# Feed-forward matmuls of a two-block Conformer kernel: one stationary operand for 512 moving columns, gate and up spread over four PSUM banks

## The reference, cut to what matters

```python
def swiglu(h, wg, wu, wd):
    return (jax.nn.silu(h @ wg) * (h @ wu)) @ wd

# first block:    x = x + first_mixer(rms_norm(x)); h = rms_norm(x, norm2_g)
#                 x = x + swiglu(h, w_gate, w_up, w_down)                  first feed-forward
# second block, each of two layers l:
#   x = x + 0.5 * rmsnorm(swiglu(rmsnorm(x, g[0]), ...), g[1])             second, fourth
#   x = x + rmsnorm(mixer(rmsnorm(x, g[2])), g[3])                         even mixer, odd mixer
#   x = x + 0.5 * rmsnorm(swiglu(rmsnorm(x, g[4]), ...), g[5])             third, fifth
```

## Time and profile before

| | before |
|---|---|
| median of 3 runs | 1394.74 us (1394.70 to 1394.78) |
| the profiled execution, its own time | 1394.34 us |
| its span, first to last instruction | 1392.5 us |
| TensorE matmuls | 1361.8 us busy, 98% of the span, 9546 of them |
| VectorE | 774.1 us, 56% |
| ScalarE | 630.3 us, 45% |
| mean granted TensorE clock | 0.992 |
| the 16 DMA engines | 169 GB/s on average |

### The profile page before, as it was taken

The page is one execution under the profiler, slowest core; times in us unless marked ns, Lnnn a source line. Parts: engine busy times, 40 slices in busy tenths (PEclk is TensorE's granted clock), DMA queues, the critical chain, the costliest instruction groups (busy, mean ns, idle before and its releaser), DMA issues.

```text
span 1392.5 us, 22880 instructions
## 1 busy us (share of the span) xinstructions
PE 1361.8 (98%) x9546; PEld 1260.9 (91%) x9546; DVE 774.1 (56%) x906; ACT 630.3 (45%) x811; POOL 86.3 (6%) x117
## 2 busy tenths in 40 slices
PE   8989999999999999999899999999999999999998
PEld 7977999999999999897799999999999998899997
DVE  6976654445644447666754444654445534654443
ACT  6654444443444334545554443454434654543331
POOL 3540000000000000000000000000002120000000
PEclk9999999999999999999999999999999999999999
DMA  8423565554655544224565555555555743465530
GB/s 266 152 91 132 188 211 181 181 182 166 212 182 185 188 145 152 92 86 134 195 221 182 181 183 179 189 204 181 185 192 170 228 119 98 166 234 190 181 121 31
DMA packets 174219, 235.17 MB, mean 169 GB/s; under 512 B 5359, under 2 KB 154111, under 8 KB 174144
## 3 DMA queue, kind: packets, MB, share of 16 engines
q1 hardware_dynamic: 170368, 223.52, 47.6%
q0 software_dynamic: 3184, 9.37, 2.2%
q10 hardware_dynamic: 592, 1.19, 0.2%
HBM read 233.03 MB, written 1.05 MB: 168 GB/s over the span
## 4 chain that ended last, share of the span: by engine, by line
PE 87%; DVE 7%; issue 2%; ACT 2%; POOL 1%; DMA 0%; DVEq 0%; POOLq 0%; ACTq 0%
PE psum L983 27%; PE psum L984 26%; PE psum L985 26%; DVE w_lo L1519 2%; PE psum L1162 1%; PE psum L1154 1%; PE psum L1153 1%; PE psum L1064 1%; DVE psum L1742 1%; ACT ws L438 1%; POOL st L857 1%; PE psum L1170 1%; PE psum L1172 1%; PE psum L1171 1%; DVE ws L1576 1%
## 5 line engine op out<-in xcount | busy, mean ns | idle before, releaser
L1519 DVE TENSOR_TENSOR w_lo<-raw,w_hi 128x2048 fp32r<-128x2048 f32 (+1 forms) x212 | 476.5, 2285 | 73.4 <-ACT w_hi L419 73.4
L983 PE MATMUL psum<-t_hi,w_hi 128*128 128x256 f32 x1472 | 419.1, 285 | 1.6 <-DVE t_lo L1586 1.6
L984 PE MATMUL psum<-t_lo,w_hi 128*128 128x256 f32 x1472 | 417.6, 284 | 0.0
L985 PE MATMUL psum<-t_hi,w_lo 128*128 128x256 f32 x1472 | 417.5, 284 | 0.0
L419 ACT ACTIVATE w_hi<-raw 128x2048 fp32r<-128x2048 f32 (+1 forms) x212 | 396.8, 1900 | 26.9 <-PE psum L985 19.7
L983 PEld LDWEIGHTS psum<-t_hi,w_hi 128*128 128x128 f32 x1472 | 283.6, 193 | 3.6 <-DVE t_lo L1586 1.9
L984 PEld LDWEIGHTS psum<-t_lo,w_hi 128*128 128x128 f32 x1472 | 283.6, 193 | 1.4
L985 PEld LDWEIGHTS psum<-t_hi,w_lo 128*128 128x128 f32 x1472 | 283.5, 193 | 0.0
L983 PE MATMUL psum<-w_hi,t_hi 128*128 128x256 f32 (+2 forms) x912 | 269.6, 296 | 5.3 <-DVE t_lo L1586 3.0
L985 PE MATMUL psum<-w_hi,t_lo 128*128 128x256 f32 (+2 forms) x912 | 265.4, 291 | 0.0
L984 PE MATMUL psum<-w_lo,t_hi 128*128 128x256 f32 (+2 forms) x912 | 265.3, 291 | 0.0
(11 more groups left out here) (166 smaller groups left out, 934.9 us busy)
## 6 DMA issues: line engine op xcount, KB each, us to landing
raw<-in_ffn_wg SPq DMA_DIRECT2D x44, 1024.0 KB, 5.2
raw<-in_ffn_wu SPq DMA_DIRECT2D x44, 1024.0 KB, 6.3
raw<-in_ffn_wd SPq DMA_DIRECT2D x44, 1024.0 KB, 6.5
raw<-in_even_w_in SPq DMA_DIRECT2D x13, 1024.0 KB, 5.2
raw<-in_odd_w_in SPq DMA_DIRECT2D x12, 1024.0 KB, 5.7
raw<-in_w_gate SPq DMA_DIRECT2D x11, 1024.0 KB, 5.2
raw<-in_w_up SPq DMA_DIRECT2D x11, 1024.0 KB, 6.3
raw<-in_w_down SPq DMA_DIRECT2D x11, 1024.0 KB, 6.7
```

The costliest lines, as they stand in the source:

```text
L983: nc.tensor.matmul(o, lh, rh, start=start, stop=False)
L984: nc.tensor.matmul(o, lh, rl, start=False, stop=False)
L985: return nc.tensor.matmul(o, ll, rh, start=False, stop=stop)
L1519: nc.vector.tensor_tensor(w_lo[:, n % SLOTS, 0:w], raw[:, n % RAWS, 0:w], w_hi[:, n % SLOTS, 0:w].bitcast(F32), ALU.subtract).then_inc(lo_ ...
```

## The change

In the chunks 2 to 9 the two matmuls that share the stationary `w_hi` become one whose moving operand is `t_hi` and `t_lo` side by side (they now lie in one tile, `t_both`): 256 + 256 columns into one whole bank. The third (`w_lo` by `t_hi`) adds to the bank's first half. So each 128-channel block has a bank of its own with two halves that still have to be added: gate takes banks 4 and 5, up takes 6 and 7, for every chunk. ACT copies the second halves to SBUF, DVE adds the first halves; silu and product then read SBUF. TensorE waits for the sum of gate (up) of chunk c-1 before it writes gate (up) of chunk c. The three splits of a chunk now stand between these steps in ACT's and DVE's programs and no longer ahead of them. In chunks 0, 1 and 10 gate and up of a chunk become one moving operand of 512 columns, for one token tile, into one bank; `turn_x` stands in the middle of the second pair.

```diff
-        t_hi = sb("t_hi", [P, KT, S], F32R)
-        t_lo = sb("t_lo", [P, KT, S], F32R)
+        t_both = sb("t_both", [P, 2, KT, S], F32R)
+        t_hi, t_lo = t_both[:, 0, :, :], t_both[:, 1, :, :]
...
+        WIDE = CHUNKS - 3
...
+            def halves_of(b):
+                v = psum[:, b:b + 2, :]
+                return v[:, :, 0:S], v[:, :, S:2 * S]
```

ScalarE's part of a chunk, and the end of its program:

```diff
+                def chunk(c, turn=0):
+                    s, k = n0 + 3 * c - 1, WIDE * ph["f"] + c - 1
                     act.wait_ge(unit_used, s + 1 + turn * SLOTS)
-                    nc.scalar.activation(f_s[:, c % 2, :], bank[4 + 2 * (c % 2)][:, :], ACT.Silu).then_inc(silu_done, 1)
-                    act.wait_ge(prod_done, 1 + PARTS * ph["f"] + c + 1 + turn * 2)
+                    nc.scalar.activation(f_b[:, 0, :, :], halves_of(4)[1], ACT.Copy).then_inc(gate_part, 1)
+                    split_hi(s + 3, turn=turn)
+                    act.wait_ge(gate_sum, k + turn * 2)
+                    nc.scalar.activation(f_s[:, c % 2, :], f_s[:, c % 2, :], ACT.Silu).then_inc(silu_done, 1)
+                    split_hi(s + 4, turn=turn)
+                    act.wait_ge(unit_used, s + 2 + turn * SLOTS)
+                    nc.scalar.activation(f_b[:, 1, :, :], halves_of(6)[1], ACT.Copy).then_inc(up_part, 1)
+                    split_hi(s + 5, turn=turn)
+                    act.wait_ge(prod_done, 1 + c0 + c + 1 + turn * 2)
                     nc.scalar.activation(f_hi[:, c % 2, :], f_p[:, c % 2, :], ACT.Copy).then_inc(prodhi_done, 1)
...
-                split_to(n0 + 29)
-                chunk(n0 + 3 * (CHUNKS - 3) - 1, CHUNKS - 3)
-                split_to(n0 + 3 * (CHUNKS - 2) + 5)
-                chunk(n0 + 3 * (CHUNKS - 2) - 1, CHUNKS - 2)
+                chunk(CHUNKS - 3)
+                chunk(CHUNKS - 2)
+                cur[0] = n0 + 3 * CHUNKS - 1
                 split_to(n0 + 3 * CHUNKS + 2)
                 last_silu(0)
```

TensorE:

```diff
+            def by_channels_wide(n, b, turn=0):
+                pe.wait_ge(lo_done, n + 1 + turn * SLOTS)
+                wh, wl = w_cols(n)
+                for c in range(2):
+                    o = bank[b + c]
+                    for k in range(KT):
+                        cs = slice(c * P, (c + 1) * P)
+                        if k < KT - 1:
+                            nc.tensor.matmul(o[:, :], wh[:, k, cs], t_both[:, :, k, :], start=k == 0, stop=False)
+                        nc.tensor.matmul(o[:, 0:S], wl[:, k, cs], t_hi[:, k, :], start=False, stop=False)
+                    mm = nc.tensor.matmul(o[:, :], wh[:, KT - 1, cs], t_both[:, :, KT - 1, :], start=False, stop=True)
+                mm.then_inc(unit_used, 1)
...
+            def by_tokens_pair(n, b, t, between=None):
+                pe.wait_ge(lo_done, n + 2)
+                ts = slice(t * P, (t + 1) * P)
+                for k in range(KT):
+                    tile_ready(t, k)
+                    if between and k == KT // 2:
+                        between()
+                    mm = three(bank[b][:, :], t_hi[:, k, ts], t_lo[:, k, ts], pair_cols(w_hi, n, k), pair_cols(w_lo, n, k),
+                               k == 0, k == KT - 1)
+                return mm
...
                 def gate_up(c, i=0):
-                    b = 4 + 2 * (c % 2)
-                    pe.wait_ge(prod_done, c0 + c + i * 2)
-                    by_channels(n0 + 3 * c - 1, b, i)
-                    by_channels(n0 + 3 * c, b + 1, i)
+                    k = WIDE * ph["f"] + c - 2
+                    if c > 2:
+                        pe.wait_ge(gate_sum, k + i * 2)
+                    by_channels_wide(n0 + 3 * c - 1, 4, i)
+                    if c > 2:
+                        pe.wait_ge(up_sum, k + i * 2)
+                    else:
+                        pe.wait_ge(prodlo_done, c0 + 2)
+                    by_channels_wide(n0 + 3 * c, 6, i)
...
-                for u in range(4):
-                    if u == 3:
-                        turn_x(ph["edge"], 1)
-                    by_tokens_tile(n0 + u, 4 + u, 0)
-                for u in range(4):
-                    if u == 3:
-                        turn_f(0, (0, 1))
-                    by_tokens_tile(n0 + u, 4 + u, 1).then_inc(unit_used, 1)
+                by_tokens_pair(n0, 4, 0)
+                by_tokens_pair(n0 + 2, 6, 0, lambda: turn_x(ph["edge"], 1))
+                by_tokens_pair(n0, 5, 1).then_inc(unit_used, 2)
+                by_tokens_pair(n0 + 2, 7, 1, lambda: turn_f(0, 0)).then_inc(unit_used, 2)
...
                 for t in range(T):
-                    by_tokens_tile(n0 + 3 * last - 1, 4, t).then_inc(unit_used if t else half_used, 1)
-                    by_tokens_tile(n0 + 3 * last, 5, t).then_inc(unit_used if t else half_used, 1)
+                    by_tokens_pair(n0 + 3 * last - 1, 4 + t, t).then_inc(unit_used if t else half_used, 2 if t else 1)
                     down(n0 + 3 * last + 1, last - 1, last - 1, tiles=(t,), rs=(0,))
-                    turn_f(last + t, (t,))
+                    turn_last(t)
                     down(n0 + 3 * last + 1, last - 1, last - 1, tiles=(t,), rs=(1,))
```

VectorE's part of a chunk:

```diff
+                def chunk(c, turn=0):
+                    s, b, k = n0 + 3 * c - 1, c % 2, WIDE * ph["f"] + c - 1
+                    halves = lambda v: v.rearrange("p (c s) -> p c s", c=2)
+                    dve.wait_ge(gate_part, k + turn * 2)
+                    nc.vector.tensor_tensor(halves(f_s[:, b, :]), halves_of(4)[0], f_b[:, 0, :, :], ALU.add).then_inc(gate_sum, 1)
+                    split_lo(s + 3, turn=turn)
+                    split_lo(s + 4, turn=turn)
+                    dve.wait_ge(up_part, k + turn * 2)
+                    nc.vector.tensor_tensor(f_b[:, 1, :, :], halves_of(6)[0], f_b[:, 1, :, :], ALU.add).then_inc(up_sum, 1)
+                    dve.wait_ge(up_sum, k + turn * 2)
                     dve.wait_ge(silu_done, c0 + c + 1 + turn * 2)
-                    dve.wait_ge(unit_used, s + 1 + turn * SLOTS)
-                    nc.vector.tensor_tensor(f_p[:, b, :], bank[5 + 2 * b][:, :], f_s[:, b, :], ALU.mult).then_inc(prod_done, 1)
+                    nc.vector.tensor_tensor(halves(f_p[:, b, :]), f_b[:, 1, :, :], halves(f_s[:, b, :]), ALU.mult).then_inc(prod_done, 1)
+                    split_lo(s + 5, turn=turn)
                     dve.wait_ge(prodhi_done, c0 + c + 1 + turn * 2)
                     nc.vector.tensor_tensor(f_lo[:, b, :], f_p[:, b, :], f_hi[:, b, :].bitcast(F32), ALU.subtract)\
                         .then_inc(prodlo_done, 1)
```

More of the change, by code:

```diff
@@ L112, in build @@
         f_p = wv(4096, 2, 512)
+        f_b = wv(2048, 2, 2, S)
         yg = wv(7168, T, D)
@@ L248, in build @@
         prod_done = sem("prod_done")
+        gate_part = sem("gate_part")
+        gate_sum = sem("gate_sum")
+        up_part = sem("up_part")
+        up_sum = sem("up_sum")
         prodhi_done = sem("prodhi_done")
@@ L500, in ffn @@
             def ffn(ph):
-                n0 = ph["n0"]
-                def chunk(s, c, turn=0):
+                n0, c0 = ph["n0"], PARTS * ph["f"]
+                def chunk(c, turn=0):
+                    s, k = n0 + 3 * c - 1, WIDE * ph["f"] + c - 1
                     act.wait_ge(unit_used, s + 1 + turn * SLOTS)
-                    nc.scalar.activation(f_s[:, c % 2, :], bank[4 + 2 * (c % 2)][:, :], ACT.Silu).then_inc(silu_done, 1)
-                    act.wait_ge(prod_done, 1 + PARTS * ph["f"] + c + 1 + turn * 2)
+                    nc.scalar.activation(f_b[:, 0, :, :], halves_of(4)[1], ACT.Copy).then_inc(gate_part, 1)
[7 more added lines that the diff above has]
+                    act.wait_ge(prod_done, 1 + c0 + c + 1 + turn * 2)
                     nc.scalar.activation(f_hi[:, c % 2, :], f_p[:, c % 2, :], ACT.Copy).then_inc(prodhi_done, 1)
                 def first_silu(c):
-                    act.wait_ge(unit_used, n0 + 2 * c + 1)
-                    nc.scalar.activation(f_s[:, c, :], bank[4 + 2 * c][:, :], ACT.Silu).then_inc(silu_done, 1)
+                    act.wait_ge(unit_used, n0 + 2 * c + 2)
+                    nc.scalar.activation(f_s[:, c, :].rearrange("p (t s) -> p t s", t=T), halves_of(4 + 2 * c)[0], ACT.Silu)\
+                        .then_inc(silu_done, 1)
                 def first_hi(c):
@@ L535, in ffn @@
                 first_hi(1)
-                whole = CHUNKS // 2 - 2
-                with act.Fori(0, whole) as i:
+                with act.Fori(0, CHUNKS // 2 - 2) as i:
                     for j in range(2):
[L539 to L542, removed]
-                split_to(n0 + 29)
-                chunk(n0 + 3 * (CHUNKS - 3) - 1, CHUNKS - 3)
-                split_to(n0 + 3 * (CHUNKS - 2) + 5)
-                chunk(n0 + 3 * (CHUNKS - 2) - 1, CHUNKS - 2)
+                        chunk(2 + j, turn=i)
+                chunk(CHUNKS - 3)
+                chunk(CHUNKS - 2)
+                cur[0] = n0 + 3 * CHUNKS - 1
                 split_to(n0 + 3 * CHUNKS + 2)
@@ L1074, in down, with turn_f @@
```

(19 more changed lines are left out.)

39 lines of the change are left out of this document (22 added, 17 removed).

## The result

The changed kernel takes 1397.72 us (median of 20 runs, 1392.49 to 1399.73) where the kernel before takes 1394.03 (20 runs, 1391.82 to 1395.76): a ratio of 1.0020, 95% interval 1.0011 to 1.0029. It is slower, by 3.7 us; 4.4 us of gain were forecast. The profiled execution took 1398.32 us against 1394.34.

What follows compares the result with a forecast made beforehand. TensorE was taken to bound the feed-forwards, by matmuls times their spacing. Gross gain 24.6 us, less 9.3 (ends), 0.9 (t = 1), 5.6 (starts) and 4.4 (clock), left 4.4: 1390.3 us, range 1377 to 1400.

Steps and rivals of the forecast that it cites:

- I take the sum of the two measured spacings: Chunks 2 to 9: a merged pair costs 0.2275 + 0.1199 = 0.3474 us, gaining 12.3 ns, 15.7 us over 1280.
- rival 2: Chunks 2 to 9: mixed widths cost more, the pair takes 0.36 us, 15.7 us vanish, 1406 us; chance 0.14.
- the one at 1019.66: Timeline row before the change: a 512-column matmul right behind a change of width takes up to 0.24 us.
- Rival 3: Joined operands of 512 columns run as two of 256, 0.2398 us; all 24.6 us stay away, 1415 us; chance 0.06.
- The Trainium skill's 2.5 ns: Rule of columns / 2.4 GHz plus about 2.5 ns per matmul; the 2000 removed would be worth 5 us.
- New wait 3.0 us: Turn at the end of the first, third and fourth feed-forward waits for the late split of n0+34; 9.0 us.
- I give two a fall: Two of the three end waits are followed by a fall of TensorE's clock, 1.6 us each, 3.2 us.
- So I add a fall, 1.2 us as part of it lies in the wait; the third has one already: Starts: the fifth feed-forward's 4.15 us wait brings a new clock fall, 1.2 us; the third gets no additional one.
- At the starts: Second pair waits for the fourth unit's split: 1.7, 4.3, 0.7, 4.15 us in feed-forwards one, three, four, five; net 5.6.
- These new waits cost nothing in chunks 2 to 9: Inside the loop, TensorE's waits for the sums of gate and up are covered: sums done well before they are needed.
- t = 1: Turn at the end of the second to fourth feed-forward waits for DVE's norm; the pair's 0.3 us is lost, 0.9 us.
- Rival 1: Seams between stages stay covered because n0+34 lands and is split sooner than chained; 1378 us; chance 0.2.

Runs made afterwards that it cites:

- e8: e4 with the chunk matmuls grouped by width per unit (14 of 512 columns, 16 of 256, 2 of 512): 1370.99 us, ratio 0.9842.
- e1: Changed kernel with each 128-channel block's matmuls reordered: seven of 512 columns, eight of 256, one of 512, not alternating: 1394.3 us, ratio 1.0003.
- e2: Changed kernel with each chunk's three splits put back ahead of the chunk's steps on ACT and DVE: 1381.57 us, ratio 0.9914.
- e5: Kernel before, narrow matmuls kept, with only the three splits of a chunk moved behind its silu on ACT and around the product on DVE: 1406.84 us, ratio 1.0092.
- e7: e2 with seven of eight 512-column matmuls reading contiguous columns of the high part, leaving the low part out: 1382.14 us (one run).
- e3: Changed kernel with chunk 1's first token half again as two tiles of 256 columns, the turn of activations between them: 1392.4 us, ratio 0.9990.
- e4: Changed kernel with the edits of e1, e2 and e3 together: 1372.41 us, ratio 0.9850.

## Why the prediction was wrong

Its direction was wrong, while nearly all its mechanisms were there: a small net of two large sums, and three terms mis-sized to the same side. The first one alone takes the net from 4.4 us faster to 0.8 slower; the other 4.5 us come from the ends and the starts.

- **"I take the sum of the two measured spacings"** is the step that failed first. 0.3474 us for the pair; measured 11.27 / 32 = 0.352. The prediction had set 0.3508 as the point from which the kernel gets slower, and called this rival 2 with 0.14; its mechanism is what happened, at a third of its price (5.2 of 15.7 us). The row that should have weighed more is the one at 1019.66: a spacing seen in a run of equal matmuls is not the one behind another width. e8 shows that the 12.3 ns per merge are there, 11.12 us for gate and up as forecast, once the widths don't alternate; e1 comes to 11.15. Rival 3, the wide matmul that costs two narrow ones, is out: pairs in chunks 0, 1 and 10 run at 0.227. In chunks 2 to 9 as they are changed, 12.3 ns a merge became 7.5.
- **The Trainium skill's 2.5 ns** per matmul ("TensorE: Matmul & The Clock Gate", section "Wait — 56ns, not 53.3ns?") is not what this case shows: e8 has 2000 - 120 matmuls fewer than before, and its chunk stretches alone are 3.21 us shorter each, 16 us for 1280 removed, 12.5 ns each.
- **"New wait 3.0 us".** Place, chain, number (three, none in the fifth) and releaser were right, and e2 and e5 show the cause from both sides. The term that was off is the load of n0+34: 5.2 us were taken, and it landed 6.3, 5.1 and 6.2 us after its issue (in the fourth 1039.88 to 1046.07). Waits of 3.9, 2.7 and 3.8 us, 10.4 in sum, stand against 9.0. Where the load took what the forecast gave it, in the third, the wait was the forecast's too. In all three that of n0+33 was still on its way at the issue, so that alone doesn't tell the longer two from the shorter one; why they took longer stays open.
- **"I give two a fall"**: three fell, some 1.7 us each, 5.1 against 3.2. With 1.1 us for the waits that makes 3.0, of which 0.3 came back as the pairs of all ten token halves saved 0.33 us each and not 0.3; 2.6 us were missed at the ends.
- **"So I add a fall, 1.2 us as part of it lies in the wait; the third has one already"**: the number of falls was right, their length was not. The low clock lasted two stretches at both starts, and cost 2.6 us at the fifth against 1.2, and 2.7 at the third where 1.7 were there before. The fifth start became 2.7 us longer against a forecast of 1.6, the third 1.2 against 0.4.
- **At the starts** the waits were right: 1.47, 4.09, 0.58 and 3.96 us by the trace, and from start to start 1.6, 4.3, 0.7 and 4.1 (forecast 1.7, 4.3, 0.7, 4.15). None in the second, as forecast: 1.19 us gained there against 1.18 for the pairs.
- **"These new waits cost nothing in chunks 2 to 9"** was right. So was t = 1, where the pair's saving is lost to the norm of t = 0: the second feed-forward's end is 0.19 us shorter, not 0.6. Of the 0.3 us forecast for its t = 0, the trace shows 0.1 from start to start.
- **The rest**, -1.3 us, lies in the even mixer, which has one fall of the clock (at 543.47) where the kernel before has two (531.83 and 545.49). No step of the prediction touched it; the kept traces of the experiments have none to two there, so it is taken as luck.

Rival 1, covered seams, is what e2 and e3 make true by edits; the changed kernel as it is doesn't have it.

## What to carry to other kernels

When a rewrite moves splits, loads or other helpers between the steps of a loop, the loop itself may not notice, but the stage behind it starts from the last iteration's places: trace the chain at the seam, where instructions that are not needed yet (here the next stage's splits) stand ahead of the one that is. Matmuls that differ in moving width are best grouped by width; the same 64 matmuls took 11.27 us in alternation and 11.12 grouped by unit. And a forecast whose net is small against its terms is decided by the ends of the ranges: a row that speaks for the worse end deserves the weight of the whole net.

## What the runs showed of the hardware

- The spacing of a matmul depends on the widths of the ones before it. By the starts in the traces (means, at a granted clock of 1.00), behind a run of 256s the first five 512s stand 0.233, 0.236, 0.228, 0.233 and 0.231 us apart and the following ones 0.227, in e1 as in the down products before the change, whatever the operand. Back at 256 columns the first two spacings are 0.113 and 0.119, then 0.120. In strict alternation the 512s keep a mean of 0.235 (single ones 0.224 to 0.241) and the 256s 0.117; in the changed kernel the down product behind it has only two slower ones, 0.235 and 0.234. Why was not tried. e7 rules out the operand's layout, and e1 has the same banks.
- Loads of 1 MB by SP's queue, from issue to landing: 5.1 us when no other was on its way (median of 96 in the kernel before; half of them between 5.0 and 5.2). With one on its way it varies: a median of 6.5 us in the kernel before and 5.7 in the changed one.
- A wait of TensorE may or may not be followed by a stretch at half clock. At the fifth start e3 and e4 both have a wait of 2.60 us by the trace; e4 has the fall and e3 has not. In e3 the end wait of the third feed-forward, 2.9 us from start to start, has none either, while in the changed kernel the one of 2.7 has. The five waits of 2.7 to 4.3 us in the changed kernel all had one in the profiled execution. The number of falls goes with the time of one and the same kernel, by some 5 us between its runs at 0.985 and at 0.990.
